# Strassen's seven products in half of the k pairs of two down-projection column chunks of a two-layer decoder trunk

## The reference

```python
D_MODEL = 2048
SEQ = 256
D_FF = 4 * D_MODEL

def squared_relu_mlp(h, w_up, w_down):
    a = jnp.square(jax.nn.relu(h @ w_up))
    return a @ w_down

def reference(...):
    for layer in range(DEPTH):
        ...
        h = rmsnorm(x, ln_mlp_g[layer])
        x = x + squared_relu_mlp(h, mlp_w_up[layer], mlp_w_down[layer])
    return x
```

## Time and profile before

| | before |
|---|---|
| device time, median of 3 runs | 2108.58 us (2107.95 to 2109.29) |
| the profiled execution | 2109.32 us, of it 2107.6 us span |
| granted TensorE clock | 1.000 of full speed |
| PE busy | 99% of the span |
| DVE busy | 57% |
| ACT busy | 47% |
| DMA, mean | 181 GB/s |

### The profile page before, as it was taken

How to read it: one execution, slowest core, us unless ns; L and a number is a source line. 1 busy time by engine, 2 the same in 40 slices (tenths; PEclk the granted TensorE clock), 3 DMA queues, 4 the chain that set the end, 5 groups by cost and what they waited for, 6 DMA issues and landing times.

```text
span 2107.6 us, 26856 instructions
## 1 busy us (share of the span) xinstructions
PE 2094.4 (99%) x10506; PEld 1775.1 (84%) x10506; DVE 1192.7 (57%) x1429; ACT 996.4 (47%) x1417; POOL 85.5 (4%) x133
## 2 busy tenths in 40 slices
PE   8999999999999999999999999999999999999999
PEld 7887888888888888888888898888888888888887
DVE  6545555565555546555555687556555555555654
ACT  5545564444344434434445676444434434443442
POOL 0000000000000000000000255000000000000000
PEclk9999999999999999999999999999999999999999
DMA  8545544555555555565655443555555556555553
GB/s 280 178 145 161 165 167 147 183 188 188 199 184 196 187 193 180 200 198 181 199 182 171 154 126 120 166 194 180 200 188 192 188 192 194 185 200 185 179 201 134
DMA packets 198477, 381.99 MB, mean 181 GB/s; under 512 B 10892, under 2 KB 17112, under 8 KB 198360
## 3 DMA queue, kind: packets, MB, share of 16 engines
q1 hardware_dynamic: 198312, 380.29, 55.2%
q10 hardware_dynamic: 48, 0.02, 0.0%
HBM read 378.19 MB, written 2.10 MB: 180 GB/s over the span
## 4 chain that ended last, share of the span: by engine, by line
PE 98%; DVE 1%; ACT 1%; DMA 0%; issue 0%; POOL 0%; SPq 0%; DVEq 0%; ACTq 0%; POOLq 0%
PE psum L1300 23%; PE psum L1231 19%; PE psum L1233 19%; PE psum L1232 19%; PE psum L1303 11%; PE psum L1364 1%; PE psum L1450 1%; PE psum L1318 0%; DVE halves L874 0%; PE psum L1427 0%; PE psum L1273 0%; PE psum L1451 0%; PE psum L1411 0%; PE psum L1412 0%; DMA x_tok<-in_x 0%; PE psum L1421 0%
## 5 line engine op out<-in xcount | busy, mean ns | idle before, releaser
L874 DVE TENSOR_TENSOR halves<-raw,halves 128x1024 fp32r<-128x1024 f32 (+1 forms) x724 | 883.1, 1225 | 741.7 <-ACT halves L590 740.4
L590 ACT CAST halves<-raw 128x1024 fp32r<-128x1024 f32 (+1 forms) x724 | 754.0, 1043 | 916.0 <-PE psum L1233 609.5
L1300 PE MATMUL psum<-h,halves 128*128 128x512 f32 x2048 | 639.8, 396 | 0.1
L1231 PE MATMUL psum<-halves,a 128*128 128x512 f32 x1340 | 525.8, 392 | 0.0
L1233 PE MATMUL psum<-halves,a 128*128 128x512 f32 x1340 | 522.2, 390 | 0.0
L1232 PE MATMUL psum<-halves,a 128*128 128x512 f32 x1340 | 521.9, 389 | 0.0
L1303 PEld LDWEIGHTS psum<-h,halves 128*128 128x128 f32 x2048 | 380.6, 188 | 86.9
L1303 PE MATMUL psum<-h,halves 128*128 128x256 f32 x2048 | 398.1, 278 | 0.0
L1300 PEld LDWEIGHTS psum<-h,halves 128*128 128x128 f32 x2048 | 314.1, 189 | 3.5 <-DVE halves L874 0.9
L1233 PEld LDWEIGHTS psum<-halves,a 128*128 128x128 f32 x1340 | 251.6, 188 | 52.6
L1231 PEld LDWEIGHTS psum<-halves,a 128*128 128x128 f32 x1340 | 251.7, 188 | 51.6 <-ACT nat L655 0.4
(11 more groups left out here) (193 smaller groups left out, 879.9 us busy)
## 6 DMA issues: line engine op xcount, KB each, us to landing
raw<-in_mlp_w_up SPq DMA_DIRECT2D x128, 1024.0 KB, 5.5
raw<-in_mlp_w_down SPq DMA_DIRECT2D x128, 1024.0 KB, 5.0
raw<-in_sf_w_in SPq DMA_DIRECT2D x45, 1024.0 KB, 5.1
raw<-in_sf_w_o SPq DMA_DIRECT2D x16, 1024.0 KB, 5.1
raw<-in_mla_w_o SPq DMA_DIRECT2D x16, 1024.0 KB, 5.0
raw<-in_mla_w_down SPq DMA_DIRECT2D x8, 1024.0 KB, 5.0
raw<-in_mla_w_ukv SPq DMA_DIRECT2D x8, 1024.0 KB, 5.2
raw<-in_mla_w_uq SPq DMA_DIRECT2D x8, 768.0 KB, 4.7
```

What stands on the lines that cost most here:

```text
L590: nc.scalar.copy(half_piece(n, 0), raw_piece(n)).then_inc(hi_done, 1)
L874: v.tensor_tensor(half_piece(n, 1), raw_piece(n), half_piece(n, 0).bitcast(F32), ALU.subtract)\
L1231: mm(bank, x_hi, hi[:, i], start=(k == 0), stop=False)
L1300: last = mm(bank, half_piece(n, 0)[:, cols], src[:, k].rearrange("p s t -> p (s t)"), start=(k == 0), stop=(k == KT - 1))
```

## The change

In seven of the eight blocks (`FAST`: all but block 3 of layer 0) the chunks c=1 and c=2 of the down projection are worked together. Their 16 k tiles are eight pairs, called quads q = 0 to 7: two k tiles by two column chunks, against two token tiles. A quad in the old way is 2 x 2 x 2 block products, 24 matmuls. In the quads 0, 2, 4 and 6 it is now Strassen's scheme in Winograd's form, seven block products, 21 matmuls (`fast_quad`); the others keep their 24 (`plain_quad`). The seven products accumulate in seven banks over the four fast quads, and the plain quads add into four of the eight.

What is added for it: sums of token blocks (`token_sums`, four operations of 128x128 at the end of each up chunk, their high half on ACT and low half on DVE into `sd`); sums of weight blocks (`weight_sums`, one operation of 128x1024 and two of 128x512 for each fast quad, on DVE); their splits as pieces of their own; and the joining of the banks (`combine`, 12 steps of 128x512 on DVE of which four are the additions into `x_tok` that L1191 did, and one copy on ACT). A block now has 72 pieces: a fast quad is the pieces `raw` (6 matmuls), `t13` (6), `t24` (6) and `b22` (3, and only 512 columns to split), a plain quad two pieces of 12. Quad 0 is pieces 40 to 43, quad 1 is 44 and 45, quad 2 is 46 to 49, quad 3 is 50 and 51, and so on; quad 7 is 62 and 63, chunk c=3 is 64 to 71. A quad takes its weights from two loads at once (`pair_loads`), and each load serves two quads.

```diff
+FAST = (True, True, True, False), (True, True, True, True)
+PLAIN_PIECES, FAST_PIECES = 64, 72
+FAST_QUADS = 0, 2, 4, 6
...
+def pair_loads(layer, l):
+    first = block_load(layer, 0) + 20 + 2 * l
+    return (first, first + 1) if first % SLOTS != SLOTS - 1 else (first + 1, first)
+def block_plan(layer, b0):
+    load = block_load(layer, b0)
+    plan = [("raw", load + j // 2, j % 2) for j in range(40)]
+    if not FAST[layer][b0]:
+        return plan + [("raw", load + j // 2, j % 2) for j in range(40, 64)]
+    for q in range(8):
+        one, two = (p + 32 * b0 for p in pair_loads(layer, q // 2))
+        if q in FAST_QUADS:
+            m = FAST_QUADS.index(q)
+            plan += [("raw", one, q % 2), ("t13", m, 0), ("t24", m, 0), ("b22", two, q % 2)]
+        else:
+            plan += [("raw", one, q % 2), ("raw", two, q % 2)]
+    return plan + [("raw", load + j // 2, j % 2) for j in range(56, 64)]
+def quad_at(q):
+    return 40 + sum(4 if p in FAST_QUADS else 2 for p in range(q))
...
+LAST_OF = {PIECES[n][1]: n for n in sorted(PIECES) if PIECES[n][0] in ("raw", "b22")}
...
+        X1, X2, X3, X4, X5, X6, X7, X8 = (psum[:, b] for b in (2, 3, 4, 7, 0, 6, 1, 5))
...
-                    sp_.wait_ge(lo_done, 2 * load - 2 * SLOTS + 2 + 2 * extra)
+                    sp_.wait_ge(lo_done, LAST_OF[load - SLOTS] + 1 + extra)
...
+                    if FAST[layer][b0]:
+                        of = {load + 32 * b0: c for load, c in zip(pair_loads(layer, l), (1, 2))}
+                        for load in sorted(of):
+                            down(load, of[load], l)
+                    else:
+                        down(load0 + 20 + l, 1, l)
...
+                    if fast:
+                        act.wait_ge(a_step, 16 * no + 4 * c + 4 + 16 * blk)
+                        nc.scalar.copy(sd[:, c, :, 0], a_sum).then_inc(sd_hi, 1)
...
+                    if fast and j == quad_at(6) + 1:
+                        act.wait_ge(pieces_used, base + quad_at(6) + 1 + FAST_PIECES * blk)
+                        nc.scalar.copy(c_sum[:, 0], X1).then_inc(x1_copied, 1)
...
+            def weight_sums(layer, b0, m, blk):
+
+                q = FAST_QUADS[m]
+                one, two = (p + 32 * b0 for p in pair_loads(layer, q // 2))
+                done = 12 * fast_no(layer, b0) + 3 * m
+                for load in (one, two):
+                    dve.wait_ge(raw_loaded[load % SLOTS], 16 * (load // SLOTS + 1) + 16 * 32 // SLOTS * blk)
+                at = q % 2 * 2 * N
+                t = t_sum[m % 2]
+                b11_b12 = raw[:, one % SLOTS:two % SLOTS + 1:two % SLOTS - one % SLOTS, at:at + N]
+                b12_b22 = raw[:, two % SLOTS, at:at + 2 * N].rearrange("p (i n) -> p i n", i=2)
+                b21 = raw[:, one % SLOTS, at + N:at + 2 * N]
+                v.tensor_tensor(t[:, 0:2], b12_b22, b11_b12, ALU.subtract).then_inc(t_step, 1)
+                dve.wait_ge(t_step, done + 1 + 12 * blk)
+                v.tensor_tensor(t[:, 2], b12_b22[:, 1], t[:, 0], ALU.subtract).then_inc(t_step, 1)
+                dve.wait_ge(t_step, done + 2 + 12 * blk)
+                v.tensor_tensor(t[:, 3], b21, t[:, 2], ALU.subtract).then_inc(t_step, 1)
...
+            def token_sums(no, c, blk):
+                done = 16 * no + 4 * c
+                y11, y21, y12, y22 = (y_buf[:, k, tt * P:(tt + 1) * P] for k in range(2) for tt in range(TT))
+                v.tensor_tensor(a_sum[:, 0], y21, y22, ALU.add).then_inc(a_step, 1)
+                v.tensor_tensor(a_sum[:, 2], y11, y21, ALU.subtract).then_inc(a_step, 1)
+                dve.wait_ge(a_step, done + 1 + 16 * blk)
+                v.tensor_tensor(a_sum[:, 1], a_sum[:, 0], y11, ALU.subtract).then_inc(a_step, 1)
+                dve.wait_ge(a_step, done + 3 + 16 * blk)
+                v.tensor_tensor(a_sum[:, 3], y12, a_sum[:, 1], ALU.subtract).then_inc(a_step, 1)
+            def token_sums_lo(no, c, blk):
+                dve.wait_ge(sd_hi, 4 * no + c + 1 + 4 * blk)
+                v.tensor_tensor(sd[:, c, :, 1], a_sum, sd[:, c, :, 0].bitcast(F32), ALU.subtract).then_inc(sd_ready, 1)
...
+            def combine(no, step, used, blk):
+
+                p1_p2, p1_p6, p1_p6_p7, c22 = (c_sum[:, i] for i in range(4))
+
+                def after(count):
+                    dve.wait_ge(combined, 10 * no + count + 10 * blk)
+                if step == 1:
+                    dve.wait_ge(x1_copied, no + 1 + blk)
+                    dve.wait_ge(pieces_used, used + FAST_PIECES * blk)
+                    v.tensor_tensor(p1_p6, X6, p1_p2, ALU.add).then_inc(combined, 1)
+                elif step == 2:
+                    after(1)
+                    v.tensor_tensor(p1_p6_p7, X7, p1_p6, ALU.add).then_inc(combined, 1)
+                elif step == 3:
+                    dve.wait_ge(pieces_used, used + FAST_PIECES * blk)
+                    v.tensor_tensor(p1_p2, X2, p1_p2, ALU.add).then_inc(combined, 1)
...
+                sums = {35: 0, 39: 1, 46: 2, 52: 3}
+                joined = {quad_at(6) + 2: (1,), quad_at(6) + 3: (2,), quad_at(7): (3,),
+                          quad_at(8): (4, 5), quad_at(8) + 1: (6,), quad_at(8) + 2: (7, 8), quad_at(8) + 3: (9,),
+                          quad_at(8) + 4: (10, 11), quad_at(8) + 5: (12,)}
+                ends = {39: 0, block_pieces(layer, b0) - 1: 3}
...
+                    if base + j + AHEAD < P_END:
+                        split_lo(base + j + AHEAD, blk)
+                    if fast and j == 33:
+                        token_sums_lo(no, 3, blk)
+                    if j in sums:
+                        weight_sums(layer, b0, sums[j], blk)
+                    for step in joined.get(j, ()):
+                        combine(no, step, base + j + 1, blk)
...
+            def product(bank, x_hi, x_lo, n, half, start, stop):
+                w_hi, w_lo = (half_piece(n, w)[:, half * N:(half + 1) * N] for w in range(2))
+                mm(bank, x_hi, w_hi, start=start, stop=False)
+                mm(bank, x_hi, w_lo, start=False, stop=False)
+                return mm(bank, x_lo, w_hi, start=False, stop=stop)
...
+            def fast_quad(n, q, added, blk):
+                first, last = q == FAST_QUADS[0], q == FAST_QUADS[-1]
+                c = q // 2
+                s1, s2, s3, s4 = (tuple(sd[:, c, i, s] for s in range(2)) for i in range(4))
+                for i, parts in enumerate((((X1, tokens(2 * q, 0), 0), (X2, tokens(2 * q + 1, 0), 1)),
+                                           ((X5, s1, 0), (X7, s3, 1)),
+                                           ((X6, s2, 0), (X4, tokens(2 * q + 1, 1), 1)),
+                                           ((X3, s4, 0),))):
+                    pe.wait_ge(lo_done, n + i + 1 + FAST_PIECES * blk)
+                    if first and i == 3:
+                        pe.wait_ge(x_added, added + 4 * blk)
+                    for bank, x, half in parts:
+                        closed = bank in (X1, X5, X6, X7)
+                        ins = product(bank, *x, n + i, half, first, last and closed)
+                    ins.then_inc(pieces_used, 1)
+            def plain_quad(n, q, blk):
+                last = q == 7
+                for i, banks in enumerate(((X2, X4), (X3, X8))):
+                    pe.wait_ge(lo_done, n + i + 1 + FAST_PIECES * blk)
+                    for half in range(2):
+                        for tt in range(TT):
+                            ins = product(banks[tt], *tokens(2 * q + half, tt), n + i, half,
+                                          banks[tt] is X8 and q == 1 and half == 0, last and half == 1)
+                    ins.then_inc(pieces_used, 1)
...
+                    if fast and c == 1:
+                        pe.wait_ge(cols_read, up0 + 4 + 4 * blk)
+                        for q in range(8):
+                            if q in FAST_QUADS:
+                                pe.wait_ge(sd_ready, 4 * no + q // 2 + 1 + 4 * blk)
+                                fast_quad(base + quad_at(q), q, added0 + 1, blk)
+                            else:
+                                plain_quad(base + quad_at(q), q, blk)
+                    if fast and c in (1, 2):
+                        continue
+                    if fast and c == 3:
+                        pe.wait_ge(combined, 10 * no + 3 + 10 * blk)
                     for j in range(8):
```

More of the change, by code:

```diff
@@ new lines, with block_base, block_load, fast_no @@
+L_MLP0 = P_MLP0 // 2
+L_MIX1 = L_MLP0 + 32 * NB
+L_MLP1 = L_MIX1 + (P_MLP1 - P_MIX1) // 2
+def block_base(layer, b0):
+    return (P_MLP0, P_MLP1)[layer] + sum(block_pieces(layer, b) for b in range(b0))
+def block_load(layer, b0):
+    return (L_MLP0, L_MLP1)[layer] + 32 * b0
+def fast_no(layer, b0):
+    return sum(FAST[0]) * layer + sum(FAST[layer][:b0])
+def pair_loads(layer, l):
+    first = block_load(layer, 0) + 20 + 2 * l
+    return (first, first + 1) if first % SLOTS != SLOTS - 1 else (first + 1, first)
@@ new lines, in quad_at, with all_pieces, put @@
```

(38 more changed lines are left out.)

186 lines of the change are left out of this document (117 added, 69 removed).

## The result

The changed kernel takes 2114.54 us (median of 9 runs, 2113.71 to 2115.40), the kernel before in the same comparison 2109.22 us (2107.95 to 2109.86). The ratio is 1.0026, 95% interval 1.0016 to 1.0037: slower by 5.3 us. The forecast was 4.4 us slower, 2113.0, with a range of 2103 to 2122. The profiled execution has a span of 2112.0 us; it is the fastest of the nine, and its span is 4.4 us longer than that of the kernel before.

A forecast was written before the change was run, and what follows sets the result against it. The prediction took PE's train of matmuls as the bound: 19.0 us saved, less 7 x 2.76 us of late places and 3 x 1.37 of layer 0 loads, gave +4.4 us on 2108.6, so 2113.0 us, range 2103 to 2122.

The forecast's parts named there:

- Removed: Fast quads on PE: 84 fewer matmuls in seven blocks at 0.2267 us each, 19.0 us saved.
- Prices: Durations read from the profile for added work, mainly on DVE: a 128x512 sum 0.69 us, a weight-sum chain 2.58.
- The rival of shorter sums: Weight sums before splits 44, 51, 57: DVE goes on after 2.0 instead of 2.58 us, giving 2103.8 us; 11%.
- that of no overlap on DVE: Each DVE operation starts only at the end of the one before, 0.09 us longer each: 2121.6 us; 5%.
- The four late places: PE waits for DVE before pieces 44, 51, 57 and 64: 1.36, 0.31, 0.31, 0.78 us, together 2.76 a block.
- The sum: Whole kernel: -19.0 us removed, 7 x 2.76 late places, 3 x 1.37 layer 0 loads, giving +4.4 us.
- the late load: Layer 0, quad 6: second load of pair 3 delays the sums, so piece 57 waits 1.68 instead of 0.31 us.
- The cover of the token sums: Up chunk's end: fourth piece ahead is split 1.1 us before PE needs it, 0.75 after the last up chunk.
- The whole saving: Rival: DVE does not delay PE at all, so all 19.0 us show, 2089.6 us; 6%.
- Later loads: Rival: paired loads land 1 us later and 3.5 us apart, quad 4's sums late too, 2119.6 us; 18%.
- a margin of 1.3: Pair of loads for quad 4: 1.3 us of room before late landings would delay its weight sums.

The follow-up runs named there:

- The load experiment: Against the changed kernel, SP issues the two loads of a pair in the order their slots come free; 2111.11 us.
- the two moves of sums: Two runs against the changed kernel: weight sums for quad 2 after split 45, 2105.35 us; those for quads 4 and 6 after splits 51 and 57, 2106.77 us.
- the move of the join: Against the changed kernel, only the third joining step is moved, ahead of the split of piece 66; 2109.43 us.

## Why the prediction was right

**Removed.** 84 matmuls at 0.2267 us. With all these waits taken away 17.6 of 19.0 us showed, 19.1 with the stand added back; the new products last as long as the old ones.

**Prices.** Sums of 128x512 took 0.69 us, of 128x1024 1.22, and DVE went on 2.59 us after a chain of three began (529.82 to 532.41), against 2.58. The rival of shorter sums and that of no overlap on DVE are both out: 531.80 to 532.41 is 0.61 for an operation that lasts 0.69. The Trainium skill (VectorE: DVE Perf Modes, Terms) has it that the next operation cannot issue before the pipe is empty; the trace agrees only for operations that wait for the one before.

**The four late places**, predicted and measured, with 0.27 added to the idle time: piece 44, 1.36 and 1.34; piece 51, 0.31 and 0.28; piece 57, 0.31 and 0.28 in layer 1, 1.68 and 1.45 to 1.55 in layer 0; piece 64, 0.78 and 0.77 on average (3.5 / 7 + 0.27). All together 11.1 + 3.5 + 17 x 0.27 for the visible ones and 11 x 0.28 for the others, 22.3 us, where 23.4 were forecast. The load experiment, the two moves of sums and the move of the join took each away alone, so these causes are shown and not only argued.

**The sum.** -19.0 + 22.3 + 1.7 for the stand = +5.0, measured +5.3. That the forecast's 4.4 lies within 1 us is partly luck, since two errors nearly cancelled: the waits were over-sized by 1.1 us, of which 0.6 is the late load (1.68 against 1.45 to 1.55, three times), and the stand, 1.7 us, was missing. Block by block the mechanism holds without the luck. From the first up matmul of a block to that of the next (of the last block, to PE's last matmul), the three changed blocks of layer 0 are 1.1 to 1.2 us longer in the trace after than in the one before (forecast 1.41), and the four of layer 1, without the stand, between 0.2 shorter and 0.2 longer (forecast +0.04). With the stand that is 5.1 us. The spans of the two traces differ by only 4.4, since PE came to the first MLP block 1.2 us earlier in the trace after, and needed 0.5 us more between the layers; neither is explained by the change.

**Mis-sized.** The cover of the token sums (1.1 us, measured 1.28) was a bound that did not bind. In the expectations, one more operation on DVE was to cost nothing and cost 2.7 us: a split that ends within the last matmul before its piece is not on time.

**The rivals.** The whole saving was given 6% for this order of work, and that it did not come is no evidence that it cannot: but for the stand it came once three weight sums and one joining step were moved. *Later loads* had 18%. The second load of quad 4's pair did land late, 7.5 us after its issue at 534.93 in block 0 of layer 0, which is 542.4 (view of DMA, then timeline of DVE):

```profile
raw<-in_mlp_w_down SPq DMA_DIRECT2D x1, 1024.0 KB, 7.5
```

```profile
543.04 1.22 DVE L1286 TENSOR_TENSOR mix<-raw 128x1024 f32<-128x1024 f32 x1
```

It was 0.6 us ahead of its sum, and 0.6 to 1.5 in the seven blocks, where the forecast had a margin of 1.3. That rival stayed out, by less than was thought.

## What to carry to other kernels

When work is added to an engine that feeds the bound engine, do not ask what share of it is busy; write down, for each item that the bound engine waits for, what stands ahead of it in the feeder's order and how long the bound engine takes to get there. Speeding up a stretch (24 matmuls to 21, in short pieces) shortens exactly these windows. Added work belongs right behind the item that is needed next, where its own consumer allows it; a later place also gave its input time to land here. The same instructions took 2114.5 us in one order and 2091.2 in another. Where two transfers go out in a fixed order on one queue, let the one whose buffer is free first go first.

## What the runs showed of the hardware that was not expected

- A wait of PE costs 0.27 us more than the idle time that the view shows (0.16 of lost overlap and 0.11 of a longer first matmul), and 0.06 to 0.16 us already when the weight load alone is held up, with no idle time of PE shown.
- Of two loads of 1 MB issued 0.65 us apart on SP's queue the first landed after 5.0 us, the second after 7.0.
- PE stood idle 1.2 to 1.7 us with no semaphore behind it, once, at the same matmul early in the second pass of the loop of layer 1, in the changed kernel and all ten kernels made from it, and not in the kernel before. It was not explained.
